# A row of maxima moved by DMA instead of through TensorE and ScalarE, and score matmuls of the next item packed into fewer steps

## The reference

```python
for blk in range(T // Q_BLOCK):
    s = einsum('bqhd,bkhd->bhqk', q[:, lo:hi], k[:, :hi]) * scale
    ...
    p = softmax(where(mask, s, -inf), axis=-1)
    outs.append(einsum('bhqk,bkhd->bqhd', p, v[:, :hi]))
```

## Time and profile before

| | |
|---|---|
| median of 3 runs | 2756.73 us (2755.0 to 2756.81) |
| profiled execution | 2759.26 us, of which the span is 2757.5 us |
| TensorE matmul busy | 2466.5 us (89% of the span) |
| VectorE, ScalarE, GpSimd busy | 45%, 35%, 33% of the span |
| the chain that ended last | 79% TensorE, 14% VectorE |
| `turn_max`: runs of four matmuls | 64 (6 before a first item in pairs, 26 pairs in all between items) |

### The profile page before, as it was taken

The page is one execution under the profiler, slowest core; times in us unless marked ns, Lnnn a source line. Parts: engine busy times, 40 slices in busy tenths (PEclk is TensorE's granted clock), DMA queues, the critical chain, the costliest instruction groups (busy, mean ns, idle before and its releaser), DMA issues.

```text
span 2757.5 us, 32825 instructions
## 1 busy us (share of the span) xinstructions
PE 2466.5 (89%) x13104; PEld 1876.4 (68%) x13104; DVE 1231.7 (45%) x1918; ACT 972.3 (35%) x1596; POOL 913.2 (33%) x786
## 2 busy tenths in 40 slices
PE   7977699997999998799999676999979999987999
PEld 7755577985587685555697455879855967855556
DVE  4059833631414325645331698255224243265553
ACT  4232215531434333244433222156214243332441
POOL 1235512222433521254411455212136235102543
PEclk9988899998999999899999888999989999998999
DMA  4100042130010111300321000522200101121003
GB/s 134 50 0 1 0 153 80 64 136 15 1 47 1 44 41 56 115 1 1 123 77 34 0 1 1 183 66 77 107 16 1 47 1 44 50 93 68 1 1 115
DMA packets 91863, 141.15 MB, mean 51 GB/s; under 512 B 18208, under 2 KB 65344, under 8 KB 91712
## 3 DMA queue, kind: packets, MB, share of 16 engines
q1 hardware_dynamic: 91712, 139.05, 14.7%
HBM read 105.48 MB, written 33.55 MB: 50 GB/s over the span
## 4 chain that ended last, share of the span: by engine, by line
PE 79%; DVE 14%; issue 2%; POOL 2%; ACT 2%; DMA 1%; POOLq 0%; SPq 0%; DVEq 0%; ACTq 0%
PE psum L227 36%; PE psum L478 12%; PE psum L1379 6%; PE psum L1364 4%; PE psum L1333 3%; PE psum L864 3%; PE psum L1367 3%; PE psum L1365 3%; PE psum L1346 2%; PE psum L1318 2%; DVE gla_E L703 2%; DVE gla_ql L666 2%; DVE gla_A L724 1%; PE psum L1386 1%; DVE gla_S L756 1%
## 5 line engine op out<-in xcount | busy, mean ns | idle before, releaser
L193 POOL TENSOR_TENSOR w_lo<-w_raw,w_hi 128x2048 fp32r<-128x2048 f32 (+3 forms) x60 | 279.3, 4656 | 907.3 <-ACT w_hi L186 907.1
L864 PE MATMUL psum<-gla_ql,gla_kl 128*128 128x256 f32 x448 | 150.7, 492 | 114.2 <-DVE gla_ql L666 110.0
L227 PE MATMUL psum<-h_hi,w_lo 128*128 128x512 f32 x768 | 193.3, 395 | 32.5 <-POOL w_lo L193 32.5
L864 PEld LDWEIGHTS psum<-gla_ql,gla_kl 128*128 128x128 f32 x448 | 107.6, 251 | 160.7 <-DVE gla_A L724 109.7
L227 PE MATMUL psum<-h_hi,w_hi 128*128 128x512 f32 x768 | 196.2, 398 | 0.0
L227 PE MATMUL psum<-h_lo,w_hi 128*128 128x512 f32 x768 | 191.0, 391 | 0.0
L227 PEld LDWEIGHTS psum<-h_hi,w_lo 128*128 128x128 f32 x768 | 146.1, 191 | 63.8 <-POOL w_lo L193 33.3
L1579 POOL TENSOR_TENSOR mla_acc<-mla_acc,mla_p 128x512 f32<-128x512 f32 (+3 forms) x160 | 153.5, 972 | 108.6 <-ACT mla_p L1447 107.8
L227 PE MATMUL psum<-w_hi,h_hi 128*128 128x256 f32 (+3 forms) x1280 | 185.1, 288 | 4.7 <-ACT w_hi L186 4.7
L227 PE MATMUL psum<-w_lo,h_hi 128*128 128x256 f32 (+3 forms) x1280 | 179.9, 283 | 4.9 <-POOL w_lo L193 4.9
L227 PE MATMUL psum<-w_hi,h_lo 128*128 128x256 f32 (+3 forms) x1280 | 181.3, 285 | 0.0
(11 more groups left out here) (323 smaller groups left out, 4847.5 us busy)
## 6 DMA issues: line engine op xcount, KB each, us to landing
w_raw<-in_w_in_dram SPq DMA_DIRECT2D x38, 1024.0 KB, 5.2
out_dram<-x_rows SPq DMA_DIRECT2D x64, 512.0 KB, 2.7
x_rows<-out_dram SPq DMA_DIRECT2D x56, 512.0 KB, 5.5
w_raw<-in_w_out_dram SPq DMA_DIRECT2D x16, 1024.0 KB, 5.2
x_first<-in_x_dram SPq DMA_DIRECT2D x8, 512.0 KB, 7.7
x_rows<-in_x_dram SPq DMA_DIRECT2D x8, 512.0 KB, 6.7
w_raw<-in_w_in_dram SPq DMA_DIRECT2D x2, 1088.0 KB, 8.8
w_raw<-in_w_in_dram SPq DMA_DIRECT2D x2, 1056.0 KB, 5.2
```

What stands on the lines that cost most here:

```text
L193: pool.tensor_tensor(self.w_lo[c["set"]][:, :n], self.w_raw[c["set"]][:, :n], self.w_hi[c["set"]][:, :n].bitcast(F32), ALU.subtract).then_ ...
L227: last = pe.matmul(o, lhs, rhs, start=(kk == 0 and n == 0), stop=(kk == KT - 1 and n == 2))
L864: last = pe.matmul(k.psum[:, n % self.NB, g * HH * self.HALF:(g + 1) * HH * self.HALF], self.kl[:, m % self.R, g, :], self.ql[:, m % self. ...
```

## The change

The maxima no longer pass through TensorE, PSUM and ScalarE. Four DMAs per head carry each a column of `nmax` (128 partitions, 4 bytes each) to 128 neighbouring places of row 96. They are issued from SP, in a loop over all items that stands in `sync_fox` behind the load of "fq0" (att1) and behind the load of "lat1" (att0), and in `sync_mla` behind three loads of x rows (attC). `nmax` is float32r now, since VectorE's write has to round. The scores of the next item go from 3 a step over six steps to 4 a step over four (c = 0), and one step earlier (c = 1).

```diff
-        self.nmax = k.at(f"{name}_nmax", small + 64, [P, self.NI, 2, 4])
+        self.nmax = k.at(f"{name}_nmax", small + 64, [P, self.NI, 2, 4], F32R)
...
+        self.m_placed = [Signal(k, f"att_m_placed{a}", 64 * N) for a in range(2)]
...
-            return range(3 * j, min(3 * j + 3, 16)) if j < 6 else range(0)
-        return range(j - 5, j - 4) if 5 <= j < 13 else range(0)
-
-    def m_at(self, i, j):
-        ...
+            return range(4 * j, 4 * j + 4) if j < 4 else range(0)
+        return range(j - 4, j - 3) if 4 <= j < 12 else range(0)
...
-    def turn_max(self, pe, i, a):            # and its calls in begin_pe and tensor
-        ...
         if j < 2:
-            pe.wait_ge(self.m_done.sem, self.m_done.at(2 * i + a + 1))
+            pe.wait_ge(self.m_placed[a].sem, self.m_placed[a].at(64 * (i + 1)))
...
-    def place_max(self, act, i, a):          # and its calls in begin_act and scalar
-        ...
+    def place_max(self, sp, i):
+        p, c = self.items[i]
+        for a in range(2):
+            if c == 0:
+                sp.wait_ge(self.max_done.sem, self.max_done.at(self.s_base[i] + 4 * (a + 1)))
+            else:
+                sp.wait_ge(self.max_joined.sem, self.max_joined.at(2 * (i // 2) + a + 1))
+            for x in range(4):
+                row = self.q_hi[(2 * p + c) % self.QS][M_ROW:M_ROW + 1, a, x * P:(x + 1) * P].bitcast(F32)
+                sp.dma_start(row, self.nmax[:, i, a, x:x + 1].bitcast(F32)).then_inc(self.m_placed[a].sem, 16)
...
     k.load_chunk(sp, L, "fq0")
+    for i in range(a.att1.NI):
+        a.att1.place_max(sp, i)
     a.att1.wait_operands(sp)
     for name in ("fk0", "fv0", "lat1"):
         k.load_chunk(sp, L, name)
+    for i in range(a.att0.NI):
+        a.att0.place_max(sp, i)
     a.att0.wait_operands(sp)
...
     for t in range(3):
         a.outC.load_row(sp, t)
+    for i in range(a.attC.NI):
+        a.attC.place_max(sp, i)
     a.attC.wait_operands(sp)
```

More of the change, by code:

```diff
@@ L1223, in __init__ @@
         n = {"blank": 2, "turned": G, "hi_done": G, "lo_done": G, "scores": T, "max_done": T, "max_joined": 2 * self.NP,
-             "m_turned": 2 * N, "m_done": 2 * N, "st_done": T, "exp_done": T, "pv_done": T, "acc_done": T, "rs_done": N,
+             "st_done": T, "exp_done": T, "pv_done": T, "acc_done": T, "rs_done": N,
              "ln_done": N, "r0_done": N, "t_done": N, "u_done": N, "scaled": N, "y_done": N}
-        (self.blank, self.turned, self.hi_done, self.lo_done, self.scores, self.max_done, self.max_joined, self.m_turned,
-         self.m_done, self.st_done, self.exp_done, self.pv_done, self.acc_done, self.rs_done, self.ln_done, self.r0_done,
+        (self.blank, self.turned, self.hi_done, self.lo_done, self.scores, self.max_done, self.max_joined,
+         self.st_done, self.exp_done, self.pv_done, self.acc_done, self.rs_done, self.ln_done, self.r0_done,
          self.t_done, self.u_done, self.scaled, self.y_done) = (Signal(k, "att_" + a, b) for a, b in n.items())
+        self.m_placed = [Signal(k, f"att_m_placed{a}", 64 * N) for a in range(2)]
         self.misc, self.misc_end = {}, []
@@ L1232, in __init__ @@
             kind, a, b = use
-            self.misc_end.append({"pre": (self.lo_done, 8 * a + b + 1), "m": (self.m_done, 2 * a + b + 1),
-                                  "rs": (self.t_done, a + 1)}[kind])
+            self.misc_end.append({"pre": (self.lo_done, 8 * a + b + 1), "rs": (self.t_done, a + 1)}[kind])
     def misc_uses(self):
         yield from (("pre", 0, g) for g in range(8))
-        yield from (("m", 0, a) for a in range(2))
         for i in range(self.NI):
@@ L1243, in misc_uses @@
                     yield ("pre", *self.pre_at(i, j))
-                if self.m_at(i, j) is not None:
-                    yield ("m", i + 1, self.m_at(i, j))
                 if i and j == 3:
@@ L1275, in scores_at @@
         if self.items[i][1] == 0:
-            return range(3 * j, min(3 * j + 3, 16)) if j < 6 else range(0)
-        return range(j - 5, j - 4) if 5 <= j < 13 else range(0)
-    def m_at(self, i, j):
-        if i + 1 == self.NI:
-            return None
-        return {5: 0, 7: 1}.get(j) if self.items[i][1] == 0 else {12: 0, 14: 1}.get(j)
+            return range(4 * j, 4 * j + 4) if j < 4 else range(0)
+        return range(j - 4, j - 3) if 4 <= j < 12 else range(0)
     def score(self, i, n):
@@ L1336, in score_pe @@
         last.then_inc(self.scores.sem, 1)
-    def turn_max(self, pe, i, a):
[L1339 to L1348, removed]
     def scores_turned(self, pe, i, j):
@@ L1395, in begin_pe @@
                 self.turn(pe, 0, groups[n // 2])
-        for a in range(2):
-            self.turn_max(pe, 0, a)
     def tensor(self, pe):
@@ L1412, in tensor @@
                     self.score_pe(pe, i + 1, n)
-                if self.m_at(i, j) is not None:
-                    self.turn_max(pe, i + 1, self.m_at(i, j))
                 if i and j == 3:
@@ L1432, in round_group @@
            .then_inc(self.hi_done.sem, 1)
-    def place_max(self, act, i, a):
[L1435 to L1438, removed]
     def exponent(self, act, i, j):
@@ L1460, in begin_act @@
             self.round_group(act, 0, g)
-        for a in range(2):
-            self.place_max(act, 0, a)
     def scalar(self, act, hook=None):
@@ L1469, in scalar @@
                     self.round_group(act, *self.pre_at(i, j))
-                if self.m_at(i, j) is not None:
-                    self.place_max(act, i + 1, self.m_at(i, j))
                 if i and j == 4:
@@ L1547, in end_dve @@
         self.out(dve, self.NI - 1)
+    def place_max(self, sp, i):
[7 more added lines that the diff above has]
+                row = self.q_hi[(2 * p + c) % self.QS][M_ROW:M_ROW + 1, a, x * P:(x + 1) * P].bitcast(F32)
+                with self.k.nc.allow_non_contiguous_dma(reason="128 maxima"):
+                    sp.dma_start(row, self.nmax[:, i, a, x:x + 1].bitcast(F32)).then_inc(self.m_placed[a].sem, 16)
     def blank_rows(self, pool, link, slots):
```

## The result

The changed kernel takes **2780.97 us** in the median of four executions (2775.63 to 2789.54), the kernel before 2755.86 us beside it: a ratio of 1.0085 (95% interval 1.0063 to 1.0107). It is slower by 25 us. The forecast was 2715 us, and the result lies outside its range. The profiled execution is the slowest of the four, 2789.54 us: its span is 30.3 us longer than before's.

A forecast was written before the change was run, and what follows sets the result against it. TensorE was taken as the bound, busy 89% of the span, waiting in the attention stages. Gains of 21 + 13 + 4 x 1.1 + 2 x 1.8 = 42 us off 2756.7 gave 2715 us; range 2690 to 2752 us.

The forecast's parts named there:

- What goes: 64 `turn_max` on TensorE's path, 0.97 us each, 62 us in all; their 64 ScalarE copies were worth nothing by themselves.
- c = 1 items: Ends of the 10 that prepare a next item: 2.1 us gained each, 21 us in all; bounds 1.9 and 2.4.
- c = 0 items: 16 items without two `turn_max`, scores spread over four steps: 0.8 us gained each, 13 us in all; +31 to -19.
- The new wait: From the last maximum to the row placed by four DMAs: 3.95 us, hidden, but barely, by the cover.
- the rival of late rows: All 32 places wait for what exceeds about 4.2 us; loses from 5.5 us on; chance 0.11 beyond break-even.
- the 7.5 us of a single DMA engine: Within the late-rows rival: one engine alone serves the row, about 7.5 us from last maximum to row; 2820 us.
- Beginnings: Starts of stages, first `scores_turned` earlier: 1.1 us gained four times in fox, 1.8 us twice in mla.
- GpSimd's order is untouched: Said beside the new wait, with no other queue losing anything; no cost was put on it.
- The clock rival: Clock falls in first four steps of c = 0 items: 16 items about 5 us more, 80 us, 2795 us; chance 0.05.
- The sum: Whole kernel: 21 + 13 + 4 x 1.1 + 2 x 1.8 = 42 us gained, giving 2715 us against the median.

The follow-up runs named there:

- begin_old: The changed kernel, but the first item of each stage gets its row from TensorE and ScalarE as before; median 2747.84 us, ratio .9944.
- first_by_dma: The kernel before, with only the rows of the six first items placed by DMA, their small matmuls and copies removed; median 2797.64 us, ratio 1.0146.
- fill_ident: The changed kernel with 12 unread float32 matmuls of 128 columns behind the last score of each beginning; median 2736.01 us, ratio .9921.
- fill_begin: The changed kernel with unread 512-wide matmuls in the six beginnings, one ahead of each score from the third, five behind the last; 2771.13 us, ratio 1.0052.

## Why the prediction was wrong

- **What goes and c = 1 items: right.** 27.25 us became 25.03 in attC, 2.22 less against 2.1. In `begin_old`, whose items have 0.4 us of half clock in all, the ten are 19.2 us shorter; 21 was forecast.
- **c = 0 items: the mechanism right, the size low.** At full clock 17.24 instead of 18.52 us, 1.28 less, and 15.30 instead of 16.87 in first items, 1.57 less; 0.8 was forecast. The reductions ended 13.4 us into item 2 (13.9 was worked out). In `begin_old` the sixteen are 22.2 us shorter, against 13.
- **The new wait: right.** 2.0 us to landing and about 4.0 us in all; the rival of late rows falls, and so does the 7.5 us of a single DMA engine (how many engines served a row was not looked at). The fixed cost that the Trainium skill gives for a DMA ("DMA: Bandwidth & Descriptors", "Anatomy of one DMA"), about 2.0 us, agrees with the landings here, though the page has it from DMAs of another issue path.
- **Beginnings: the step that failed.** "the first `scores_turned` starts then instead of at 691.01: 1.1 us gained, 4 times" came true to 0.1 us in att1. From the first score of a beginning to the item, the six are 0.6 to 2.1 us shorter, 8.2 us in all against 8.0 forecast. But it was counted as if the item behind stayed as it was. What the sum left out is what the removed matmuls did there: they stood on the path, and in fox they were the dense work behind which the clock came back; without them the four items begin at half clock and are 24 us longer than before. In attC the clock came back without them, but fell 3 us into the item, 11 us longer in two. 12 of the 64 `turn_max` cost, when taken away, 44 us in the first items (`first_by_dma`). The prediction had read the fall at 686.97 and the return at 690.6, and the rows had the `turn_max` between them (688.08 to 690.79), but it asked only whether the clock would fall anew, not what had brought it back.
- **"GpSimd's order is untouched": true, and not enough.** The order stayed, but the weight split in it now comes later against TensorE's last item of a fox stage, and the row sums wait 2.4 us for GpSimd, 9.5 us in the four stages. The sum had nothing for it.
- **The clock rival was the outcome, and given .05.** It put 80 us on 16 items because of their own pattern of scores. Measured against `begin_old`'s faster profile, the changed kernel's 67 us more are 44.6 us in the six first items, 16.4 in four of the other ten, 2.5 in c = 1 items and 3.5 in the rest. Of these, 30.1 us lie in fox's first items, which began at half clock, and 30.9 in attC's first items and those four, where the clock fell inside the item, as the rival said. Its "in item 2 the same pattern of scores and waits held 1.00" is true, but was read at one item of the kernel before. The Trainium skill ("TensorE: Matmul & The Clock Gate", "What's actually happening") says that the clock is throttled by default and that activity releases it, which the prediction weighed for that rival. The beginning of att1 agrees, with the clock back at .91 behind the `turn_max` and at .50 without them; the changed kernel's first item does not, busy for 22.31 of 24.09 us and at .50 throughout.
- **The sum at full clock** was 42 us: the faster profile of `begin_old` is 36.7 us shorter than before's (19.2 + 22.2 in items, less 4.7 in the rest), at 2722.6 us. That is near the forecast of 2715, but in part by luck. This kernel lacks the 8 us of the beginnings, its c = 0 items won 9 us more than forecast, its row sums lose the 9.5 us, and the stretches ahead of att1 in both layers, which the change hardly touches, are 8.6 us shorter in this profile. Its median is 2747.84 us.

The stretches from the start of the last item of att1 and att0 to the next stage's first item (107.6 and 236.7 us before) are 4 us longer each even in `begin_old` (111.6 and 240.7), but not in `first_by_dma` (108.0, 235.0). The 2.4 us of the row sums' wait are in them, and none in `first_by_dma`; in `begin_old` they also hold more half clock (10.0 us instead of 3.4 behind att1). No run took that wait away. What stays open is what decides between `begin_old`'s two ways through attC, why wide matmuls did not bring the clock back in att1, and what makes a full clock fall inside some c = 0 items, attC's first ones above all.

The best version by median is `fill_ident`, 2736.0 us, ratio .9921 (.9897 to .9944): the change, with 72 matmuls that nobody reads.

## What to carry to other kernels

Work on TensorE that looks like pure cost may be what brings its clock back. Before removing matmuls at the start of a stage, read the granted clock there by short stretches, and if it returns behind them, price the stage behind at half clock: here 5 to 9 us for each first item (`first_by_dma`) against 0.6 to 2.1 us saved in its beginning. And when a change makes a stage slower while every wait is as expected, compare the same stretch of the program at its own clock before looking for a new wait.

## What the runs showed that was not expected

- TensorE busy by the profile for 4.00 of 4.00 us (ends of matmuls are modelled) with 12 matmuls, mostly 512 columns wide, left the clock at .50 (`fill_begin`, att1, the last 0.7 us in item 0). Being busy did not bring it back there.
- Once at half, the clock could stay there long although TensorE was busy: 22.31 of 24.09 us in the changed kernel's first item of att1, all at .50.
- The same kernel ran at 2722.6 and at 2749.9 us, .952 and .936 of the clock, and two profiles, one of each group, put the largest part of their difference into attC's first items.
- Moving 128 words from 128 partitions to one took .601 us to issue and 2.0 us to land (1.9 to 3.3), for all 256 DMAs of the kernel.
